# Two-layer decoder step on one core: the sorted index scores turned inside a projection unit, and one merge over 128 partitions in place of two over 64

## The reference, cut to what matters

```python
dots = jnp.einsum('bqhd,bkd->bqhk', bqi, ki).astype(F32)
score = jnp.einsum('bqh,bqhk->bqk', bwi.astype(F32) * idx_scale, jax.nn.relu(dots))
score = jnp.where(mask[None], score, -jnp.inf)
_, idx = lax.top_k(score, n_sel)        # 256 of 1088 keys (sample), 64 of 256 (prompt)
...
p = jax.nn.softmax(jnp.where(valid[:, :, None, None, :], s, -jnp.inf), axis=-1)
```

## Time and profile before

| what | us |
|---|---|
| median of 3 runs (lowest to highest) | 1387.71 (1387.58 to 1388.55) |
| the profiled execution's own time | 1387.57 |
| its span, first to last instruction | 1385.9 |
| PE busy, DVE busy, ACT busy, POOL busy | 1226.8, 483.7, 345.9, 89.9 |
| mean granted TensorE clock (1 is full speed) | 0.952 |

### The profile page before, as it was taken

One profiled execution on the slowest core, in us unless ns is written; L12 is line 12 of the kernel. 1 busy time (PEld: TensorE's weight loads), 2 busy tenths in 40 slices (PEclk: granted clock), 3 DMA queues, 4 the chain that ended last, 5 costly groups with the idle time before them and its releaser, 6 DMA issues.

```text
span 1385.9 us, 21400 instructions
## 1 busy us (share of the span) xinstructions
PE 1226.8 (89%) x7403; PEld 623.3 (45%) x7404; DVE 483.7 (35%) x1048; ACT 345.9 (25%) x755; POOL 89.9 (6%) x155
## 2 busy tenths in 40 slices
PE   8998888888969999988799983999978999988885
PEld 3445666665533333333355442665553333333332
DVE  1012545554441011111551947444252111111154
ACT  1112434344011121111123232555211111211111
POOL 2000000000100000000412240000100000000010
PEclk9998999999979999999899995999988999999988
DMA  9864989958539799999735102436645989999831
GB/s 346 362 228 147 353 331 356 347 225 299 179 155 396 291 403 399 402 401 404 241 99 189 60 12 69 122 119 237 219 182 186 383 304 405 402 402 400 298 120 39
DMA packets 144224, 364.30 MB, mean 263 GB/s; under 512 B 14832, under 2 KB 31248, under 8 KB 138784
## 3 DMA queue, kind: packets, MB, share of 16 engines
q1 hardware_dynamic: 134128, 327.74, 63.7%
q0 software_dynamic: 7344, 26.83, 5.5%
q10 hardware_dynamic: 2688, 8.91, 1.7%
HBM read 341.48 MB, written 21.97 MB: 262 GB/s over the span
## 4 chain that ended last, share of the span: by engine, by line
PE 62%; SPq 9%; DVE 8%; DMA 4%; issue 3%; ACT 3%; POOL 0%; DVEq 0%; ACTq 0%; POOLq 0%
PE PS L990 11%; SPq L422 8%; PE PS L1011 6%; PE PS L1188 5%; PE PS L1145 5%; PE PS L903 5%; PE PS L934 5%; PE PS L793 4%; DMA ring<-in_moe_w_up 3%; PE PS L847 2%; PE PS L806 2%; PE PS L1395 1%; PE PS L993 1%; PE PS L1356 1%; PE PS L973 1%
## 5 line engine op out<-in xcount | busy, mean ns | idle before, releaser
L990 PE MATMUL PS<-ring,QKV 128*64 128x512 f32 (+1 forms) x512 | 227.9, 593 | 22.3 <-DMA ring<-in_moe_w_up 18.5
L993 PE MATMUL PS<-ring,QKV 128*64 128x512 f32 (+1 forms) x512 | 228.0, 594 | 0.0
L1445 ACT ACTIVATE QKV<-PS 128x512 f32<-128x512 f32 (+4 forms) x180 | 95.1, 528 | 372.4 <-PE PS L1011 106.1
L990 PEld LDWEIGHTS PS<-ring,QKV 128*64 128x64 f32 (+1 forms) x512 | 70.4, 140 | 165.2 <-issue 157.6
L1011 PE MATMUL PS<-ring,QKV 128*64 128x512 f32 (+1 forms) x512 | 123.8, 598 | 0.2
L934 PE MATMUL PS<-X,QKV 128*64 128x512 f32 x432 | 103.3, 613 | 3.1 <-DVE QKV L2155 3.1
L2164 DVE TENSOR_TENSOR QKV<-QKV,PS 64x512 f32<-64x512 f32 (+1 forms) x32 | 21.8, 680 | 228.5 <-ACT QKV L1608 228.5
L702 PE MATMUL PS<-ring,XT 128*128 128x512 f32 (+1 forms) x320 | 87.7, 489 | 0.0
L2169 DVE COPY QKV<-PS 64x512 f32<-64x512 f32 (+1 forms) x32 | 22.2, 693 | 186.4 <-PE PS L1011 186.4
L1445 ACT ACTIVATE KP<-PS 128x512 f32<-128x512 f32 (+1 forms) x114 | 64.5, 579 | 81.0 <-PE PS L793 51.0
L1445 ACT ACTIVATE XT<-PS 128x512 f32<-128x512 f32 (+4 forms) x128 | 50.9, 447 | 122.2 <-PE PS L669 57.4
(11 more groups left out here) (318 smaller groups left out, 1437.5 us busy)
## 6 DMA issues: line engine op xcount, KB each, us to landing
ring<-in_moe_w_gate SPq DMA_DIRECT2D x64, 1024.0 KB, 14.4
ring<-in_moe_w_up SPq DMA_DIRECT2D x64, 1024.0 KB, 14.5
ring<-in_moe_w_down SPq DMA_DIRECT2D x32, 2048.0 KB, 15.6
ring<-in_cache_a_k SPq DMA_DIRECT2D x64, 512.0 KB, 6.8
ring<-in_cache_a_v SPq DMA_DIRECT2D x64, 512.0 KB, 7.4
ring<-in_a_w_in SPq DMA_DIRECT2D x5, 2048.0 KB, 24.3
places<-OR POOLq DMA_DIRECT2D x8, 1024.0 KB, 16.9
ring<-in_ple_gate_w SPq DMA_DIRECT2D x4, 2048.0 KB, 17.3
```

Source lines behind the costliest of these rows:

```text
L990: ins = pe.matmul(PS[0:m, 0, :], XE[:, k, 0:m], wg[:, k, :], start=(k == 0), stop=(k == KD - 1))
L993: ins = pe.matmul(PS[p1:p1 + m, 1, :], XE[:, k, 0:m], wu[:, k, :], start=(k == 0), stop=(k == KD - 1))
L1445: ins = act.activation(dst, src, ACT.Copy) if scale is None else \
```

## The change

The transposes of `SORTED` move from behind unit 14 into unit 12 on PE, between its contraction chunks 5 and 6, with the wait for the end of the sort ahead of them. They write PSUM bank 7. The reversal matmuls follow at once behind unit 12; there are now four, which bring each half reversed to the partitions of the other, in bank 6. ACT's copy moves ahead of its emptying of unit 12. DVE merges both halves at once over 128 partitions: the first operation in two halves of 64 partitions with two comparisons, then six over 128 partitions; the copy of two columns goes. SP, ahead of kb1, waits for `rotated1` 3 as well as for `selection`, as `selection` no longer comes behind POOL's last use of the scratch in that slot.

```diff
@@ SP
                             s = place((what, pr))
+                            if item((what, pr))[0] == item(("b_in", 4))[0] + SLOTS:
+                                sp.wait_ge(*at("rotated1", 3))
@@ PE
+            def sorted_turn():
+                pe.wait_ge(*at("sorted", SEL_SAMPLE // 8))
+                for c in range(2):
+                    ins = pe.transpose(PS[:, 7, 128 * c:128 * c + 128], SORTED[:, 128 * c:128 * c + 128], ident)
+                ins.then_inc(S("sort_mm"), 1)
+
+            def sorted_reverse():
+                pe.wait_ge(*at("sort_evac", 1))
+                for c in range(2):
+                    for half in range(2):
+                        ins = pe.matmul(PS[NS * half:NS * half + NS, 6, 128 * c:128 * c + 128],
+                                        TURNED_SORTED[:, 1 - c, NS * (1 - half):NS * (1 - half) + NS], cst("reversal"),
+                                        start=True, stop=True)
+                ins.then_inc(S("sort_mm"), 1)
+
-            def unit(n):
+            def unit(n, between=lambda: None):
...
                 for k in range(KD):
+                    if k == 6:
+                        between()
...
             for n in range(10, 14):
-                unit(n)
+                if n == 12:
+                    unit(n, sorted_turn)
+                    sorted_reverse()
+                else:
+                    unit(n)
...
-            pe.wait_ge(*at("sorted", SEL_SAMPLE // 8))
-            for c in range(2):
-                ins = pe.transpose(PS[:, 4, 128 * c:128 * c + 128], SORTED[:, 128 * c:128 * c + 128], ident)
-            ins.then_inc(S("sort_mm"), 1)
-            pe.wait_ge(*at("sort_evac", 1))
-            for c in range(2):
-                ins = pe.matmul(PS[0:NS, 5, 128 * c:128 * c + 128], TURNED_SORTED[:, 1 - c, NS:P], cst("reversal"),
-                                start=True, stop=True)
-            ins.then_inc(S("sort_mm"), 1)
@@ ACT
             for n in range(10, 14):
+                if n == 12:
+                    act.wait_ge(*at("sort_mm", 1))
+                    copy(TURNED_SORTED, PS[:, 7, 0:256].rearrange("p (c r) -> p c r", c=2), "sort_evac")
                 unit(n)
...
-            act.wait_ge(*at("sort_mm", 1))
-            copy(TURNED_SORTED, PS[:, 4, 0:256].rearrange("p (c r) -> p c r", c=2), "sort_evac")
@@ DVE
-            first, second = SORTED[0:NS, :], PS[0:NS, 5, 0:SEL_SAMPLE]
-            taken, other = PICK[0:NS, 0:SEL_SAMPLE], PICK[0:NS, SEL_SAMPLE:2 * SEL_SAMPLE]
-            for rank, (values, least, ties) in enumerate((
-                    (first, LEAST[0:NS], TIES[0:NS]), (second, small[0:NS, 150:151], small[0:NS, 151:152]))):
-                link(ve.tensor_tensor(taken, first, second, ALU.is_ge if rank == 0 else ALU.is_lt))
...
-            link(ve.tensor_copy(small[NS:P, 148:150], small[0:NS, 150:152]))
+            taken, other = PICK[:, 0:SEL_SAMPLE], PICK[:, SEL_SAMPLE:2 * SEL_SAMPLE]
+            for half, keep in enumerate((ALU.is_ge, ALU.is_gt)):
+                rows = slice(NS * half, NS * half + NS)
+                ins = ve.tensor_tensor(taken[rows], SORTED[rows, :], PS[rows, 6, 0:SEL_SAMPLE], keep)
+            link(ins)
+            link(ve.tensor_scalar(other, taken, -1.0, PICKED, ALU.add, ALU.mult))
+            link(ve.tensor_tensor(taken, taken, SORTED, ALU.mult))
+            link(ve.tensor_tensor(other, other, taken, ALU.add))
+            link(ve.tensor_reduce(LEAST, other, AX.X, ALU.min))
+            link(ve.tensor_scalar(other, other, LEAST, None, ALU.is_equal))
+            link(ve.tensor_reduce(TIES, other, AX.X, ALU.add))
```

## The result

The changed kernel takes 1379.32 us (median of 4 runs, 1376.99 to 1381.48), the kernel before 1387.64 beside it (4 runs, 1386.96 to 1388.55): a ratio of 0.9939, interval 0.992 to 0.9959. It is faster, by some 8.3 us. The forecast was 12.8 and its range ended at 1378.4, so the sign was right and the size was not. The profiled execution of after is its slowest run: 1381.48 us, span 1379.8, against 1387.57 and 1385.9 before.

A forecast was written before the change was run, and what follows sets the result against it. PE's late turn left DVE's merge and rounds bare, with SP's page issues a second clock. Batches 15.4 us earlier, capped at 7.4 + 6.0 = 13.4, less 0.6 clock loss: 12.8 off 1387.57, 1374.8; range 1371.2 to 1378.4.

The forecast's parts named there:

- The stall and its price: PE inside unit 12 waits 6.15 us for the sort's end; with turn, reversal and clock loss, PE is 8.7 later.
- a loss of 1.88: PE behind the unit 12 stall: about 3 us at the lower clock, costing 1.88 us.
- The merge and DVE: DVE merge starts at 818.3, takes 3.4 us for 6.07, then waits for POOL; batch 0 starts 15.4 earlier.
- The table load: ACT's 1.28 us load for the first exponential, covered before, now up to 1.6 us bare at batch 0.
- SP needs 16.7 to 17 us per item without a wait in between: SP's issue pace for key and value pages from kb1 on; SP was to start 7.4 us earlier.
- the slack of 6.0 us: Before the change kb3 lands at 936.5 and PE asks for it in batch 5 at 942.50.
- second clock loss: PE's wait for kb3 in batch 5 may drop the clock again: 0 to 1.88 us, taken as 0.6.
- The rest moves as a block: Behind the batches all waits are for slots that PE frees, so everything there shifts together.
- The prefetch isn't felt: Rival, 1372.2 us, chance 0.13: PE's clock doesn't drop, SP gains 9.3 and the cap rises to 15.3.
- POOL is slowed: Rival, 1377.7 us, chance 0.07: POOL's rotation beside DVE's rounds is slowed, taking 2.9 us off the cap.
- Slower: Rival, 1391 us, chance 0.05: PE's clock stays down from the stall through units 12 to 14.
- No change: Rival, 1387.6 us, chance 0.04: the gain is given back waiting for weights in layer 1's experts.

The follow-up runs named there:

- the second profile: The changed kernel run and profiled once more, unedited: 1379.52 us, ratio 0.9942 to the kernel before.
- With the stall filled: Changed kernel plus 66 idle transposes of the identity on PE ahead of the turn's wait for the sort: 1379.24 us, ratio 0.9937.
- the run with two merges: Changed kernel with the former two merges over 64 partitions in place of the one over 128: 1378.82 us, ratio 0.9927.
- the two edits to the pages: Each against the changed kernel: POOL's rotation scratch moved out of kb1's slot, 1374.20 us; value pages vb1 to vb3 issued by POOL instead of SP, 1373.21 us.
- unit 13 with two merges: Changed kernel with the turn in unit 13 and the former two merges over 64 partitions: 1368.72 us, ratio 0.9876.

## Why the prediction was wrong in size and right in kind

*The stall and its price.* The place and the kind are as forecast. The stall itself costs nothing beyond the sort's end; that it was 7.71 and not 6.15 comes from PE arriving earlier and the sort ending later. **The first step that failed is "a loss of 1.88"**: I took the price of the low clock from a gap of 1.48 us for a stall four times as long. Behind the stall the low clock lasted some 5.5 us instead of 3 (5.2 in the second profile, behind 6.03). From the turn to the end of the scores behind unit 12 it took 821.64 - 814.96 = 6.68, where the forecast's prices at full clock give 0.22 + 1.72 + 0.45 + 1.31 = 3.70: 2.98 lost, not 1.88. With the stall filled, at full clock, the same work took 818.72 - 814.68 = 4.04, so 2.64 of the loss is the clock and 0.34 prices that were too low. SP, which hangs on the rotation behind all this, started 33.24 - 27.17 = 6.07 earlier against the sort instead of 7.4: 1.33 lost.

*The merge and DVE.* Start at 820.23 for 818.3, for the same reason and because the sort ended 0.91 later; length, the wait for POOL (3.93) and its worth of nothing are as forecast, and the run with two merges shows it. Batch 0, 14.1 earlier from the sort for 15.4, falls short by about the 1.10 that this work took beyond the 1.88 set down for it.

*The table load.* It lies bare as said: load at 847.57, 1.28 us, the exponentials right behind it. The Trainium skill, "ScalarE: Activation LUTs", section "What ACT_TABLE_LOAD costs", has a drain of 1.38 beside the load; the trace has none there, since ACT's copy ends at 847.55 and the first exponential begins 0.01 after the load:

```profile
846.95 0.60 ACT L1458 ACTIVATE KP<-PS 128x512 f32<-128x512 f32 x1 [1.11 <-PE PS L1359]
847.57 1.28 ACT L1507 ACT_TABLE_LOAD   x1
848.86 0.40 ACT L1507 ACTIVATE XT<-XT,small 128x128 f32<-128x128 f32 x1
```

*SP.* **The second step that failed is "SP needs 16.7 to 17 us per item without a wait in between"**, and with it the slack of 6.0 us. (From the start of one item to the next it was 17.45 to 17.80 even in the profile that I read; the sum uses the times themselves and not this pace.) Over eleven profiles kb1 to kb3 takes 70.81 to 73.13, and the profile I read was the shortest of the eleven; the other ten have 72.05 in the mean. Kernels with and without the change lie in the same spread (71.92 and 71.88 without it), so there is no sign that the change slows SP: I read the most favourable execution. After's own profile is the longest, 2.32 over the one I used. Three single issues of 0.85, 1.17 and 1.07 us in place of 0.33 make 2.1 of it; the profile of before that I read has none over 0.34.

*The sum, step by step, in the profiled execution.* 12.8 - 1.33 (kb1 later) - 2.32 (SP's pace) - 0.24 (second clock loss 0.84 for 0.6) + 0.13 (the late fall of the clock, 1.41 before and 1.28 after) = 9.04; measured in the stage 8.95. With the mean pace, 1.24 in place of 2.32, it would have been some 10.1. The late fall had no place in the forecast; that it struck both profiles, and so cancels, is luck.

*"The rest moves as a block"* holds for the waits: PE waits six times for the expert weights in layer 1, 9.0 us in all before and 8.8 after. It doesn't hold for single executions, whose part from projection to end was 398.5 to 402.6 over the profiles, and 407.3 with the stall filled, where PE pauses once for 4.4 us in the experts. So the two spans differ by 6.1 and the medians by 8.3; the stage's 8.95 against the first profile of before, and 7.7 against the second, enclose the difference of the medians.

*The rivals.* "The prefetch isn't felt" fell with the wait of 4.54, although it is what the two edits to the pages reach (1374.20 and 1373.21, beside its 1372.2). "POOL is slowed" fell: the rotation beside DVE's rounds has its old durations.

```profile
837.56 0.54 POOL L532 TENSOR_TENSOR ring<-QKV,C 128x160 f32<-128x160 f32 x1 [4.23 <-ACT QKV L1458]
```

It holds elsewhere: in unit 13 with two merges the rotation fell beside the end of DVE's mask and not beside its rounds, and there its first three operations took 1.11, 1.06 and 1.07 for 0.54, 0.54 and 0.90. kb1 went out 831.06 - 813.29 = 17.77 behind the turn, against 831.80 - 815.39 = 16.41 with one merge.

```profile
825.07 1.11 POOL L532 TENSOR_TENSOR ring<-QKV,C 128x160 f32<-128x160 f32 x1 [4.28 <-ACT QKV L1458]
```

"Slower" fell with the clock at 0.96 from 820 on, before unit 13. "No change" fell with the time. None of them named an item's pace that varies by 2 us from one execution to the next. That is the missing rival, and it would have widened the range upward, to 12.8 - 1.3 - 2.3 = 9.2 off, 1378.5, and with a second clock loss of 1.9 to 1379.8.

## What to carry to other kernels

When a step is moved ahead, ask what the next load into its buffer waits for, and treat a queue that issues loads one by one as a second clock of its own, whose slack is read from several executions and not from one. Put a moved step where its input is ready by then: one unit later, this turn had no stall, no low clock behind it and no late pages, and the time went from 1379.32 to 1366.94. A shorter piece of work shows only where nothing else ends last: the same merge was worth nothing in unit 12 and 3.4 us of DVE's path in unit 13.

## What the runs showed of the hardware that was not expected

*The low clock's price differs from stall to stall.* 7.71 us idle were followed by some 5.5 us at 0.50, 6.03 us (the second profile of after) by some 5.2, 1.48 us by about 3. The stalls ahead of kb3 show no such order: 4.54, 3.75 and 3.53 us idle cost 0.84, 0.90 and 0.94 (after, again, two merges), and 3.81 us cost 3.4 in the run with the filled stall. 66 transposes that nobody needs held the clock at 1.00 through the first stall.

*SP's issues stretch at odd places.* An issue of 0.33 us took up to 1.17:

```profile
885.03 1.17 SPq L478 DMA_DIRECT2D ring<-in_cache_b_k  x1
```

In that stretch of after, 884 to 886, the DMA view has two fetches of instructions (0.02 and 0.01 MB) on queues of their own. The three long issues in after, at 852.17, 885.03 and 901.13, each come within two us of one of 0.02 MB, but three more such fetches between 842 and 942 have no long issue behind them; the cause was not tried and stays open.

*DVE's mask is slowed by POOL, at a place I had not looked at.* The two operations of lines 2332 and 2333 (128x576, one scalar per partition) took 0.82 and 0.98 beside POOL's additions, 0.52 and 0.51 in the kernel before, where POOL was idle, and 0.52 and 0.52 with two merges in unit 12, where POOL's additions fall elsewhere. After's POOL there:

```profile
823.59 1.62 POOL L564 TENSOR_TENSOR OR<-SM,OR 128x256 f32<-128x256 f32 x2 [0.42 <-ACT SM L1459]
```

The Trainium skill, "SBUF — State Buffer", section "Who interferes with whom", says that such an operation can take the port pair that GpSimd needs, and that whoever comes second is blocked; the trace agrees, with DVE as the one that mostly waits, 0.77 us in all (POOL's two additions took 1.62 for 1.53). In after it is hidden by the wait for POOL's last addition; with the turn in unit 13 it lies on DVE's path.
